# Moving SBUF tiles to 512-byte addresses, and summing the squares of a retention head on the vector engine

## The chip, the core and the metric

The kernel runs on one core of a Trainium2 chip. Its engines are TensorE (PE in the rows below; PEld is its loading of stationary operands), VectorE (DVE), ScalarE (ACT), GpSimd (POOL) and SyncE (SP), which issues most transfers. Each has its own queue of instructions, worked off in order, and they meet only at semaphores. The metric is the device time of one execution in microseconds; the median of three runs of the kernel before is 2727.9 us.

## What is computed

The reference is a trunk of four layers over 256 latent and 256 context tokens of width 1024. Layers 0 and 3 mix tokens with differential attention, layer 1 with a two-way retention of four heads, layer 2 with neighbourhood attention. Behind each mixer stands a SwiGLU network of hidden width 2816. What the change touches most is the end of a retention head:

```python
def _rms(x):
    return x32 * lax.rsqrt(jnp.mean(x32 * x32, axis=-1, keepdims=True) + EPS)
...
    def finish(o, g):
        T = o.shape[1]
        o = _rms(o).reshape(B, T, H * dv).astype(g.dtype)
        return (jax.nn.silu(g) * o) @ w_o
```

So the output `o` of a head (512 channels for each of 512 tokens) is divided by the root of its mean square and multiplied by the SiLU of a gate.

## The kernel before

All activations lie transposed: channels on the 128 partitions, tokens along the row. Weights come as a stream of 424 units of 128x1024 numbers through a ring of four slots (`RING`). For each unit SP loads `w_raw`, ACT rounds it to `w_hi` (`conv`, line 794), POOL forms the remainder `w_lo = w_raw - w_hi` (line 446), and PE multiplies in three steps, hi x hi, hi x lo and lo x hi (`three`). A unit is 8 k-tiles, so 24 matmuls of type fp32r, 512 columns wide (256 in most of layer 3). ACT may convert a unit only when PE has used the one four before it (`unit_used`), and PE takes a unit only when `lo_ready` says that POOL is done.

The stages of a layer follow one another: norm, mixer, `project`, norm, `ffn`. In the matmuls of q, k, v, gate and of the first half of the FFN the activations are `h_hi`, `h_lo`. In `project` they are `y_hi`, `y_lo` (layers 0, 2, 3) or `ry_hi`, `ry_lo` (layer 1), and in the second half of the FFN `u_hi`, `u_lo`.

A retention head (`retention`, once for each engine) is a loop of four trips with 12 units each. The order on PE is written by hand: units 0 to 3 give q and k, 4 to 7 give v, then come the scores, unit 8 and 9 (gate rows 0 and 1), the 16 products of scores and values `sT`, `rv` into banks 4 to 7, unit 10 (gate row 2), four products of the squares with a tile of ones that add up the mean square in bank 1, and unit 11 (gate row 3) into bank 3. ACT squares each of the four output tiles into one of two halves of `tmp` (line 973), converts a weight unit, takes the root as `Ln` and `Exp` (`rsqrt`, lines 813 and 814), and then loads the table of SiLU and evaluates the gates (`gate`, line 984). `gate(0)` reads bank 3, which unit 8 has filled, so unit 11 cannot write there before it. DVE forms the product in `gated` (lines 1376 and 1378).

A matmul of plain fp32 (scores, values, ones) is two records in the trace, one of fp32r is one.

SBUF tiles are laid out in the order in which they are declared. The compiled program puts `w_raw`, `w_hi`, `w_lo`, `xT`, `h_hi` and `h_lo` at addresses that leave 128 when divided by 512. Behind them stand small tiles, and so `lnm`, `ssum_rstd` and `tmp` leave 288, and `u_hi`, `u_lo`, `y_hi`, `y_lo`, `ry_hi`, `ry_lo`, `rv`, `sT`, `ada_raw` and all that share their place leave 96 (`bias`, `n_x` and `nT` leave 352). `w_*` and `h_*` thus start at a multiple of 64 bytes, the tiles behind them 32 bytes off one.

Of the kernel before, what the change touches and what calls it, by code (L numbers as in the profile page):

```python
# [127 lines left out]
class Layer:  # L128


    def __init__(self, sem, li, first_unit):
        self.li, self.kind, self.par = li, KINDS[li], li % 2
        self.n, self.nf = first_unit, first_unit + MIXER_UNITS[self.kind]

        self.zq = li < DEPTH - 1
        self.W = TOK if self.zq else SEQ
        self.na = self.kind == 2
        self.da = sum(k == 0 for k in KINDS[:li])
        self.banks = 6 if self.zq else 4
        self.groups = (3 if self.zq else 2) * (2 if self.na else 1)  # L140

        self.v_done = sem(f"v_done_{li}")
        self.v_act = sem(f"v_act_{li}")
        self.v_dve = sem(f"v_dve_{li}")
        self.s_done = sem(f"s_done_{li}")
        self.osq_ready = sem(f"osq_ready_{li}")
        self.oms_done = sem(f"oms_done_{li}")
        self.ors_ready = sem(f"ors_ready_{li}")
        self.y_ready = sem(f"y_ready_{li}")
        self.y_hi_ready = sem(f"y_hi_ready_{li}")  # L150
        self.y_lo_ready = sem(f"y_lo_ready_{li}")
        if self.kind == 1:

            self.darg_ready = sem(f"darg_ready_{li}")
            self.dexp_ready = sem(f"dexp_ready_{li}")
            self.rot_ready = sem(f"rot_ready_{li}")
            self.zcopy_ready = sem(f"zcopy_ready_{li}")
            self.sT_ready = sem(f"sT_ready_{li}")
            self.o_done = sem(f"o_done_{li}")
            self.silu_g = sem(f"silu_g_{li}")  # L160
        else:

            self.qk_dve = sem(f"qk_dve_{li}")
            self.qk_act = sem(f"qk_act_{li}")
            self.negmax = sem(f"negmax_{li}")
            self.e_ready = sem(f"e_ready_{li}")
            self.a_ready = sem(f"a_ready_{li}")
            self.t_done = sem(f"t_done_{li}")
            self.aT_ready = sem(f"aT_ready_{li}")
            self.vst_ready = sem(f"vst_ready_{li}")  # L170
            self.pv_done = sem(f"pv_done_{li}")

        self.silu_ready = sem(f"silu_ready_{li}")
        self.u_free = sem(f"u_free_{li}")
        self.u_hi_ready = sem(f"u_hi_ready_{li}")
        self.u_lo_ready = sem(f"u_lo_ready_{li}")
        self.out_done = sem(f"out_done_{li}")


def trunk(nc, xT_in, cond_in, weights, ada_w, ada_b, gains, final_g, lam_in, subln_in, decay_in,  # L180
          rpb_in, da_rope_in, ret_rope_in, ret_exp_in, na_mask_in, ident_in, out, layers=DEPTH):
    with ExitStack() as ctx:  # L182
# [4 lines left out]
            return ctx.enter_context(nc.semaphore(name))  # L187


        w_raw = sb("w_raw", [P, RING, D])  # L190
        w_hi = sb("w_hi", [P, RING, D], F32R)
        w_lo = sb("w_lo", [P, RING, D], F32R)

        xT = sb("xT", [P, KT, TOK])
        h_hi = sb("h_hi", [P, KT, TOK], F32R)
        h_lo = sb("h_lo", [P, KT, TOK], F32R)

        mod = sb("mod", [P, 2, MOD, 2])
        amp = sb("amp", [P, 2, 2, KT, 2])
        ada_sum = sb("ada_sum", [P, LOOPED, 2])  # L200
# [2 lines left out]
        gain_f = sb("gain_f", [P, KT])  # L203
        eps_c = sb("eps_c", [P, 1])
        one_c = sb("one_c", [P, 1])

        ones = sb("ones", [P, P])
        ident = sb("ident", [P, P])
        lnm = sb("lnm", [P, TOK])
        ssum_rstd = sb("ssum_rstd", [P, 2, TOK])  # L210
        ssum, rstd = ssum_rstd[:, 0, :], ssum_rstd[:, 1, :]
# [1 line left out]

        lam_sb = rstd[:, :].rearrange("p (l a d) -> p l a d", l=2, a=4)
        lam_pr = lnm[:, 0:4 * DA_DIM].rearrange("p (l a d) -> p l a d", l=2, a=2)
        lam_sum = sb("lam_sum", [P, 2, 2])
        neg_lam = sb("neg_lam", [P, 2])
        subln = sb("subln", [P, 2])
        logit = sb("logit", [P, 2 * RET_HEADS])
        lg_t = sb("lg_t", [P, 4, 2 * RET_HEADS])  # L220
        log_g = sb("log_g", [P, 2, RET_HEADS])
        lg_cur = sb("lg_cur", [P, 2])

        with ExitStack() as s:
            u_hi = sb("u_hi", [P, JT, TOK], F32R, s)
# [225 lines left out]
        def _(pe):  # L451
# [214 lines left out]
            def retention(L, q):  # L666
                with pe.Fori(0, RET_HEADS) as h:
# [36 lines left out]
                    for e in range(ET):  # L704
# [1 line left out]
                            mov, w = (sT[:, 0, kb * SEQ:kb * SEQ + SEQ], SEQ) if kb < 2 else (sT[:, kb - 1, :], TOK)  # L706
                            last = mm(bank[4 + e][:, 0:w], rv[:, kb, e * P:e * P + P], mov, j == 0, j == 3)
                        last.then_inc(L.o_done, 1)
                    head_unit(10, 2)
                    for e in range(ET):  # L710

                        pe.wait_ge(L.osq_ready, h * ET + (e + 1))
                        mm(bank[1][:, :], ones[:, :], tmp[:, e % 2, :], e == 0, e == ET - 1).then_inc(L.oms_done, 1)

                    pe.wait_ge(L.y_ready, h * ET + (ET + 1))
                    head_unit(11, 3)

            def ffn(L, q):
# [58 lines left out]
        def _(act):  # L777
# [167 lines left out]
            def retention(L):  # L945
                with own.loop(RET_HEADS, 1) as h:
# [21 lines left out]
                    for e in range(ET):  # L968
                        act.wait_ge(L.o_done, h * ET + (e + 1))
                        if e >= 2:  # L970

                            act.wait_ge(L.oms_done, h * ET + (e - 1))
                        nc.scalar.activation(tmp[:, e % 2, :], bank[4 + e][:, :], ACT.Square).then_inc(L.osq_ready, 1)
                    hconv(10)
                    act.wait_ge(L.oms_done, h * ET + ET)
                    rsqrt(TOK, bank[1][:, :], RET_V, L.ors_ready)

                    def gate(e):
# [11 lines left out]
                                             tmp[:, e % 2, :], ACT.Copy).then_inc(L.y_hi_ready, 1)  # L990

                    gate(0)
                    gate(1)
                    high(0)
                    gate(2)
# [86 lines left out]
        def _(dve):  # L1082
# [248 lines left out]
            def retention(L):  # L1331
                with own.loop(RET_HEADS, 5 + ET) as h:
# [28 lines left out]
                    for g in range(3):  # L1361
# [5 lines left out]
                                               scalar=RET_QK ** -0.5, in1=dec, op0=ALU.mult, op1=ALU.mult)\  # L1367
                            .then_inc(L.sT_ready, 1)

                    def gated(e):  # L1370

                        dve.wait_ge(L.ors_ready, h + 2)
# [8 lines left out]
                    def low(e):  # L1381
                        dve.wait_ge(L.y_hi_ready, h * ET + (e + 1))
                        V.tensor_tensor(out=row(ry_lo, h * ET + e, TOK), in0=tmp[:, e % 2, :],
                                        in1=row(ry_hi, h * ET + e, TOK), op=ALU.subtract).then_inc(L.y_lo_ready, 1)

                    gated(0)
                    for e in range(1, ET):
                        gated(e)
# [196 lines left out]
```

## Time and profile before

| | us |
|---|---|
| median of 3 runs | 2727.9 |
| lowest, highest | 2727.09, 2731.14 |
| profiled execution | 2732.85 |
| its span, first to last instruction | 2730.4 |
| PE busy in it | 2451.4 (90%) |
| DVE, POOL, ACT busy | 1344.7, 1023.0, 924.2 |

The rows come from the profiled execution. It is 4.95 us (0.18%) above the median, of which 2.45 us lie outside the span. A busy PE says that a matmul was in flight, not that it ran at its best: how many matmuls start in a stretch tells more. The granted clock is 1.00 at 2.4 GHz and 0.50 at 1.2 GHz.

### The profile page before, as it was taken

To read this page: it belongs to the slowest core of one execution; us is meant where nothing else is said; L and a number is where in the kernel's file an instruction comes from. 1 tells how busy PE (TensorE), PEld (TensorE's weight loads), DVE (VectorE), ACT (ScalarE), POOL (GpSimd) and SP (SyncE) were. 2 spreads that over 40 slices of the span, in tenths; PEclk is the share of its full clock that TensorE was granted. 3 is DMA by queue.
4 is the path that set the end of the run, shared out by engine and by line. 5 is a ranking of instruction groups with operands and counts; after the bars stand their busy time and mean duration, and the time that the engine had idled before them with its cause. 6 is when DMAs were issued, how large, how long until landed. Compare 5 with 4: busy or idle time off the path is not lost.

```text
span 2730.4 us, 34462 instructions
## 1 busy us (share of the span) xinstructions
PE 2451.4 (90%) x11378; PEld 1958.4 (72%) x11378; DVE 1344.7 (49%) x2238; ACT 924.2 (34%) x1485; POOL 1023.0 (37%) x431
## 2 busy tenths in 40 slices
PE   0639989999989999998999989999999998887998
PEld 0526668887866777686887867776788786666998
DVE  7996657664141232115766113554766513466441
ACT  2215543222232233223222223553322222354553
POOL 1212223444432332243444433223344443333786
PEclk9869999999989999999999999999999998998999
DMA  7331125554221221123655327221555422222454
GB/s 284 146 139 47 50 78 209 207 186 146 93 84 58 84 74 58 60 92 135 227 194 190 100 85 131 71 84 47 208 204 197 164 96 77 77 69 86 161 169 131
DMA packets 116393, 341.27 MB, mean 125 GB/s; under 512 B 34928, under 2 KB 36208, under 8 KB 115696
## 3 DMA queue, kind: packets, MB, share of 16 engines
q1 hardware_dynamic: 108304, 335.01, 35.9%
q10 hardware_dynamic: 8032, 5.52, 1.4%
q8 instruction: 34, 0.56, 0.1%
q14 instruction: 23, 0.19, 0.0%
HBM read 335.80 MB, written 4.69 MB: 125 GB/s over the span
## 4 chain that ended last, share of the span: by engine, by line
issue 70%; POOL 26%; PE 3%; POOLq 1%; DVE 0%; ACT 0%; DVEq 0%
POOL w_lo L446 26%; PE low_banks L453 2%; PE high_banks L453 1%; POOLq L442 0%; POOLq L445 0%; DVE xT L1507 0%; POOLq L446 0%; DVE ssum_rstd L1163 0%; DVE xT L1149 0%; ACT tmp L810 0%; ACT lnm L813 0%; ACT ssum_rstd L814 0%; DVEq L182 0%; POOL ones L439 0%; POOL eps_c L440 0%
## 5 line engine op out<-in xcount | busy, mean ns | idle before, releaser
L446 POOL TENSOR_TENSOR w_lo<-w_raw,w_hi 128x1024 fp32r<-128x1024 f32 x424 | 1022.6, 2422 | 1685.9 <-ACT w_hi L794 1685.6
L453 PE MATMUL low_banks<-h_hi,w_hi 128*128 128x512 f32 (+1 forms) x1664 | 624.5, 375 | 47.6 <-DVE h_lo L1187 23.2
L794 ACT ACTIVATE w_hi<-w_raw 128x1024 fp32r<-128x1024 f32 x424 | 444.5, 1055 | 551.2 <-PE low_banks L453 261.8
L453 PE MATMUL low_banks<-h_lo,w_hi 128*128 128x512 f32 (+1 forms) x1664 | 618.6, 372 | 0.0
L453 PE MATMUL low_banks<-h_hi,w_lo 128*128 128x512 f32 (+1 forms) x1664 | 617.6, 371 | 0.0
L453 PEld LDWEIGHTS low_banks<-h_hi,w_hi 128*128 128x128 f32 x1664 | 319.5, 192 | 115.8 <-issue 53.3
L1099 DVE SCALAR_TENSOR_TENSOR ssum_rstd<-ada_raw,high_banks 128x1024 f32<-128x1024 f32 x288 | 351.2, 1220 | 29.4 <-DMA ada_raw<-in_ada_w 20.6
L453 PEld LDWEIGHTS low_banks<-h_lo,w_hi 128*128 128x128 f32 x1664 | 319.7, 192 | 52.8 <-issue 1.0
L453 PEld LDWEIGHTS low_banks<-h_hi,w_lo 128*128 128x128 f32 x1664 | 319.2, 192 | 52.7
L1014 ACT ACTIVATE lnm<-low_banks 128x512 f32<-128x512 f32 (+1 forms) x88 | 47.8, 543 | 419.6 <-PE low_banks L453 419.6
L453 PE MATMUL high_banks<-h_hi,w_hi 128*128 128x512 f32 (+1 forms) x384 | 146.1, 381 | 14.6 <-DVE v_all L1208 9.5
L1149 DVE SCALAR_TENSOR_TENSOR xT<-low_banks,mod,xT 128x256 f32<-128x256 f32 (+1 forms) x64 | 27.8, 476 | 248.4 <-PE low_banks L453 248.4
L1416 DVE TENSOR_TENSOR tmp<-low_banks,lnm 128x512 f32<-128x512 f32 (+1 forms) x88 | 55.0, 625 | 192.5 <-ACT lnm L1014 188.5
L453 PE MATMUL high_banks<-h_lo,w_hi 128*128 128x512 f32 (+1 forms) x384 | 143.6, 374 | 0.0
L453 PE MATMUL high_banks<-h_hi,w_lo 128*128 128x512 f32 (+1 forms) x384 | 143.4, 374 | 0.0
L453 PE MATMUL low_banks<-w_hi,h_hi 128*128 128x512 f32 x192 | 79.1, 412 | 70.9 <-DVE h_lo L1187 50.7
L453 PE MATMUL high_banks<-u_hi,w_hi 128*128 (+2 forms) x352 | 130.7, 371 | 7.1 <-DVE ssum_rstd L1099 7.1
L453 PE MATMUL high_banks<-u_hi,w_lo 128*128 (+2 forms) x352 | 130.6, 371 | 0.0
L453 PE MATMUL high_banks<-u_lo,w_hi 128*128 (+2 forms) x352 | 130.4, 370 | 0.0
L453 PE MATMUL low_banks<-u_hi,w_hi 128*128 (+2 forms) x352 | 129.2, 367 | 0.0
L453 PE MATMUL low_banks<-u_hi,w_lo 128*128 (+2 forms) x352 | 129.2, 367 | 0.0
L453 PE MATMUL low_banks<-u_lo,w_hi 128*128 (+2 forms) x352 | 129.2, 367 | 0.0
(177 smaller groups left out, 3596.5 us busy)
## 6 DMA issues: line engine op xcount, KB each, us to landing
w_raw<-in_weights SPq DMA_DIRECT2D x424, 512.0 KB, 3.4
ada_raw<-in_ada_w SPq DMA_DIRECT2D x144, 512.0 KB, 3.9
ada_rest<-in_ada_w SPq DMA_DIRECT2D x8, 2048.0 KB, 7.9
ada_first<-in_ada_w SPq DMA_DIRECT2D x4, 2048.0 KB, 14.5
bias<-rpb_skew SPq DMA_DIRECT2D x64, 64.0 KB, 2.4
rpb_skew<-rpb_rows ACTq DMA_DIRECT2D x1, 3556.0 KB, 38.4
cond_l<-in_cond SPq DMA_DIRECT2D x3, 1024.0 KB, 4.6
xT<-in_xT SPq DMA_DIRECT2D x1, 2048.0 KB, 14.4
```

What stands on the lines that cost most here:

```text
L446: nc.gpsimd.tensor_tensor(out=w_lo[:, r, :], in0=w_raw[:, r, :], in1=w_hi[:, r, :], op=ALU.subtract).then_inc(lo_ready, 1)
L453: return nc.tensor.matmul(dst, lhsT, rhs, start=start, stop=stop, **kw)
L794: nc.scalar.activation(w_hi[:, r, :], w_raw[:, r, :], ACT.Copy).then_inc(hi_ready, 1)
L1014: nc.scalar.activation(lnm[:, 0:L.W], bank[2 * s][:, 0:L.W], ACT.Silu)\
L1099: last = V.scalar_tensor_tensor(out=dump, in0=w, scalar=1.0, in1=cond[:, c, :], op0=ALU.mult, op1=ALU.mult, accum_out=ada_sum[:, r, c:c + 1])
L1149: last = V.scalar_tensor_tensor(out=x, in0=src[:, c * SEQ:c * SEQ + SEQ], scalar=gate_of(L, which, m, c), in1=x, op0=ALU.mult, op1=ALU.add)
L1416: V.tensor_tensor(out=tmp[:, s, 0:L.W], in0=bank[2 * s + 1][:, 0:L.W], in1=lnm[:, 0:L.W], op=ALU.mult).then_inc(L.u_free, 1)
```

## The change

There are three edits.

1. The order of declaration: the small tiles come first, then 32 bytes of padding (`before_weights`), then the large ones. `lg_t` moves into an idle part of `lnm`. In the compiled program every large tile now starts at a multiple of 512 bytes (`bias`, `n_x`, `n_z` and `nT` at 256 beyond one).
2. In a retention head DVE adds up the four squares in `ssum` (`add_output_square`, three additions), and PE multiplies once by ones, in the middle of unit 10. ACT waits for the addition and no longer for a product before it reuses half of `tmp`.
3. ACT converts the weight unit `hconv(10)` behind the root and behind `gate(0)`, and PE's unit 11 waits for `gate(0)` itself (`silu_g`) and no longer for `gated(0)` on DVE (`y_ready`).

```diff
+        sb("before_weights", [P, 8])
+        w_raw = sb("w_raw", [P, RING, D])
...
+        lg_t = lnm[:, 4 * DA_DIM:4 * DA_DIM + 8 * RET_HEADS].rearrange("p (k a) -> p k a", k=4)
...
-                    head_unit(10, 2)
-                    for e in range(ET):
-
-                        pe.wait_ge(L.osq_ready, h * ET + (e + 1))
-                        mm(bank[1][:, :], ones[:, :], tmp[:, e % 2, :], e == 0, e == ET - 1).then_inc(L.oms_done, 1)
-
-                    pe.wait_ge(L.y_ready, h * ET + (ET + 1))
+                    unit(h * 12 + (L.n + 10), L.n + 10, bank[2], H, TOK, tiles=range(3), stop=False)
+
+                    pe.wait_ge(L.osum_step, h * (ET - 1) + (ET - 1))
+                    mm(bank[1][:, :], ones[:, :], ssum[:, :], True, True).then_inc(L.oms_done, 1)
+                    unit(h * 12 + (L.n + 10), L.n + 10, bank[2], H, TOK, tiles=range(3, KT)).then_inc(unit_used, 1)
+
+                    pe.wait_ge(L.silu_g, h * ET + 1)
                     head_unit(11, 3)
...
                         if e >= 2:

-                            act.wait_ge(L.oms_done, h * ET + (e - 1))
+                            act.wait_ge(L.osum_step, h * (ET - 1) + 1)
                         nc.scalar.activation(tmp[:, e % 2, :], bank[4 + e][:, :], ACT.Square).then_inc(L.osq_ready, 1)
-                    hconv(10)
-                    act.wait_ge(L.oms_done, h * ET + ET)
+                    act.wait_ge(L.oms_done, h + 1)
                     rsqrt(TOK, bank[1][:, :], RET_V, L.ors_ready)
...
                     gate(0)
+                    hconv(10)
                     gate(1)
...
+                    def add_output_square(e):
+
+                        dve.wait_ge(L.osq_ready, h * ET + (e + 1))
+                        if e == 1:
+                            ins = V.tensor_tensor(out=ssum[:, :], in0=tmp[:, 0, :], in1=tmp[:, 1, :], op=ALU.add)
+                        else:
+
+                            dve.wait_ge(L.osum_step, h * (ET - 1) + (e - 1))
+                            ins = V.tensor_tensor(out=ssum[:, :], in0=ssum[:, :], in1=tmp[:, e % 2, :], op=ALU.add)
+                        ins.then_inc(L.osum_step, 1)
...
+                    for e in range(1, ET):
+                        add_output_square(e)
                     gated(0)
```

On PE, at the end of a retention head in the kernel before, from the last products of `sT` and `rv` to unit 11 (the names in brackets are semaphores of layer 1):

```order
L453 MATMUL high_banks<-sT,rv 128x256 x2
L467 REGISTER_ALU
L453 MATMUL low_banks<-h_hi,w_hi 128x512 [waits lo_ready]
...
L453 MATMUL low_banks<-h_hi,w_lo 128x512
L712 REGISTER_ALU
L453 MATMUL low_banks<-tmp,ones 128x512 [waits osq_ready_1] x4
L715 REGISTER_ALU
L467 REGISTER_ALU [waits y_ready_1]
L453 MATMUL low_banks<-h_hi,w_hi 128x512 [waits lo_ready]
```

The same place on PE in the changed kernel:

```order
L456 MATMUL high_banks<-sT,rv 128x256 x2
L470 REGISTER_ALU
L456 MATMUL low_banks<-h_hi,w_hi 128x512 [waits lo_ready]
...
L456 MATMUL low_banks<-h_hi,w_lo 128x512
L456 MATMUL low_banks<-ssum_rstd,ones 128x512 [waits osum_step_1]
L456 MATMUL low_banks<-h_hi,w_hi 128x512 [waits lo_ready]
...
L718 REGISTER_ALU
L470 REGISTER_ALU [waits silu_g_1]
L456 MATMUL low_banks<-h_hi,w_hi 128x512 [waits lo_ready]
```

The product with ones has moved from behind unit 10 to behind its ninth matmul, there is one of it and no longer four, and unit 11 waits for ACT's SiLU.

On ACT, at the same place in the kernel before, from the last square to the second gate:

```order
L973 ACTIVATE tmp<-high_banks 128x512 [waits oms_done_1,o_done_1]
...
L794 ACTIVATE w_hi<-w_raw 128x1024 [waits unit_used]
L813 ACTIVATE lnm<-low_banks,eps_c 128x512 [waits oms_done_1]
...
L814 ACTIVATE ssum_rstd<-lnm 128x512 [waits act_own]
...
L984 ACT_TABLE_LOAD [waits unit_used]
L984 ACTIVATE lnm<-low_banks 128x512 [waits ors_ready_1]
L984 ACTIVATE darg<-low_banks 128x512 [waits unit_used]
```

And in the changed kernel:

```order
L976 ACTIVATE tmp<-high_banks 128x512 [waits osum_step_1,o_done_1]
L816 ACTIVATE lnm<-low_banks,eps_c 128x512 [waits oms_done_1]
...
L817 ACTIVATE ssum_rstd<-lnm 128x512 [waits act_own]
...
L986 ACT_TABLE_LOAD [waits unit_used]
L986 ACTIVATE lnm<-low_banks 128x512 [waits ors_ready_1]
...
L797 ACTIVATE w_hi<-w_raw 128x1024 [waits unit_used]
L986 ACTIVATE darg<-low_banks 128x512 [waits unit_used]
```

The conversion of a weight unit has moved from ahead of the root to between the first and the second gate.

## Rows read from the trace of the kernel before

**Rows 1.** The profile's page: span, busy time of each engine, granted clock in 40 slices.

```profile
span 2730.4 us, 34462 instructions
PE 2451.4 (90%) x11378; PEld 1958.4 (72%) x11378; DVE 1344.7 (49%) x2238; ACT 924.2 (34%) x1485; POOL 1023.0 (37%) x431
PEclk9869999999989999999999999999999998998999
```

**Rows 2.** Waits of PE during the four heads (788 to 1156 us): total, times, longest.

```profile
PE low_banks L453 <- DVE tmp L1378: 16.6, 4, 4.2
```

**Rows 3.** Timeline of PE, head 0: start us, length, instruction, idle before it.

```profile
851.00 10.48 PE L453 MATMUL high_banks<-sT,rv 128*128 128x512 f32 x32
861.13 0.58 PE L453 MATMUL low_banks<-h_hi,w_hi 128*128 128x512 f32 x1
...
866.78 3.75 PE L453 MATMUL low_banks<-tmp,ones 128*128 128x512 f32 x8
...
869.40 0.30 PEld L453 LDWEIGHTS low_banks<-tmp,ones 128*128 128x128 f32 x2 [0.56 <-ACT tmp L973]
...
874.68 0.79 PE L453 MATMUL low_banks<-h_hi,w_hi 128*128 128x512 f32 x1 [4.15 <-DVE tmp L1378]
```

**Rows 4.** Timeline of ACT, head 0.

```profile
853.78 0.60 ACT L973 ACTIVATE tmp<-high_banks 128x512 f32<-128x512 f32 x1 [1.52 <-PE high_banks L453]
856.36 0.60 ACT L973 ACTIVATE tmp<-high_banks 128x512 f32<-128x512 f32 x1 [1.98 <-PE high_banks L453]
...
867.90 0.60 ACT L973 ACTIVATE tmp<-high_banks 128x512 f32<-128x512 f32 x1 [10.94 <-PE low_banks L453]
868.76 0.60 ACT L973 ACTIVATE tmp<-high_banks 128x512 f32<-128x512 f32 x1 [0.26 <-PE low_banks L453]
869.25 1.05 ACT L794 ACTIVATE w_hi<-w_raw 128x1024 fp32r<-128x1024 f32 x1
870.57 0.69 ACT L813 ACTIVATE lnm<-low_banks,eps_c 128x512 f32<-128x512 f32 x1 [0.27 <-PE low_banks L453]
871.29 0.63 ACT L814 ACTIVATE ssum_rstd<-lnm 128x512 f32<-128x512 f32 x1
871.93 1.28 ACT L984 ACT_TABLE_LOAD   x1
873.23 0.60 ACT L984 ACTIVATE lnm<-low_banks 128x512 f32<-128x512 f32 x1
```

**Rows 5.** Timelines of DVE and POOL, head 0.

```profile
871.95 0.69 DVE L1376 TENSOR_TENSOR ssum_rstd<-high_banks,ssum_rstd 128x512 f32<-128x512 f32 x1 [30.96 <-ACT ssum_rstd L814]
873.86 0.69 DVE L1378 TENSOR_TENSOR tmp<-ssum_rstd,lnm 128x512 f32<-128x512 f32 x1 [1.22 <-ACT lnm L984]
...
852.33 2.35 POOL L446 TENSOR_TENSOR w_lo<-w_raw,w_hi 128x1024 fp32r<-128x1024 f32 x1 [3.05 <-ACT w_hi L794]
870.38 2.35 POOL L446 TENSOR_TENSOR w_lo<-w_raw,w_hi 128x1024 fp32r<-128x1024 f32 x1 [15.70 <-ACT w_hi L794]
```

**Rows 6.** Windows at the slow clock: length, PE busy (count), granted clock, DMA share, GB/s.

```profile
874.68:879.85 5.17, 5.17 (x12) 0.50 0.18 72
965.95:972.01 6.06, 6.06 (x14) 0.50 0.14 56
1057.62:1060.75 3.13, 3.13 (x7) 0.50 0.26 105
1147.92:1152.92 5.00, 5.00 (x12) 0.50 0.17 67
```

**Rows 7.** Windows in stages without a wait, same columns.

```profile
660.00:760.00 100.00, 100.00 (x431) 1.00 0.29 95
1160.00:1240.00 80.00, 80.00 (x344) 1.00 0.25 85
420.00:640.00 220.00, 219.68 (x969) 1.00 0.57 203
815.00:830.00 15.00, 15.00 (x68) 1.00 0.38 125
2656.00:2716.00 60.00, 60.00 (x509) 1.00 0.46 149
2611.00:2616.00 5.00, 5.00 (x44) 1.00 0.44 154
```

**Rows 8.** One addition of squares beside POOL, behind the FFN of layer 0 (timeline).

```profile
776.76 2.42 DVE L1163 TENSOR_TENSOR ssum_rstd<-ssum_rstd,tmp 128x512 f32<-128x512 f32 x1 [0.71 <-ACT tmp L810]
776.28 2.34 POOL L446 TENSOR_TENSOR w_lo<-w_raw,w_hi 128x1024 fp32r<-128x1024 f32 x1 [3.27 <-ACT w_hi L794]
```

More of the change, by code:

```diff
@@ L160, in __init__ @@
             self.silu_g = sem(f"silu_g_{li}")
+            self.osum_step = sem(f"osum_step_{li}")
         else:
@@ L187, in sem @@
             return ctx.enter_context(nc.semaphore(name))
[L190 to L196, printed above, removed]
         mod = sb("mod", [P, 2, MOD, 2])
@@ L208, in trunk @@
         ident = sb("ident", [P, P])
+        lam_sum = sb("lam_sum", [P, 2, 2])
+        neg_lam = sb("neg_lam", [P, 2])
+        subln = sb("subln", [P, 2])
+        logit = sb("logit", [P, 2 * RET_HEADS])
+        log_g = sb("log_g", [P, 2, RET_HEADS])
+        lg_cur = sb("lg_cur", [P, 2])
+        sb("before_weights", [P, 8])
+        w_raw = sb("w_raw", [P, RING, D])
+        w_hi = sb("w_hi", [P, RING, D], F32R)
+        w_lo = sb("w_lo", [P, RING, D], F32R)
+        xT = sb("xT", [P, KT, TOK])
+        h_hi = sb("h_hi", [P, KT, TOK], F32R)
+        h_lo = sb("h_lo", [P, KT, TOK], F32R)
         lnm = sb("lnm", [P, TOK])
@@ L215, in trunk @@
         lam_pr = lnm[:, 0:4 * DA_DIM].rearrange("p (l a d) -> p l a d", l=2, a=2)
[L216 to L222, printed above, removed]
+        lg_t = lnm[:, 4 * DA_DIM:4 * DA_DIM + 8 * RET_HEADS].rearrange("p (k a) -> p k a", k=4)
         with ExitStack() as s:
```

## The prediction, made before the changed kernel ran

> **What bounds the kernel now.** I read the page first: PE has a matmul in flight for 2451.4 of 2730.4 us, and no other engine is busy for half of the span [rows 1]. So a change helps if it shortens PE's own stream, fills one of its gaps, or keeps its clock up. I then asked for PE's waits within the retention heads. There is one kind: unit 11 waits four times for `gated(0)`, 4.15 us each [rows 2, 3]. The timeline of a head shows what lies in front of that wait. Third, I laid windows over stretches in which PE never stops, and counted matmuls: that gives the pitch from one start to the next, which a busy share of 100% hides [rows 7].
>
> **The end of a head, before.** From the first matmul of unit 10 (861.13) to the first of unit 11 (874.68) are 13.55 us [rows 3]. Unit 10 is 24 matmuls at 0.2268 us, 5.44 us. The other 8.1 us are four products with ones, which ACT's third and fourth square must come between (`tmp` has two halves, and PE comes to the first product only behind unit 10, so the third square starts at 867.90 after 10.94 us of idling), and then the chain weight conversion, `Ln`, `Exp`, table, SiLU, `gated(0)` [rows 3 to 5].
>
> **The same place, after.** The products of `sT` and `rv` still end at 861.13. The squares no longer wait for PE: they follow the four outputs, 2.58 us apart [rows 4], so at about 853.8, 856.4, 858.9 and 861.5. DVE, idle for 30.96 us here [rows 5], adds at about 857.0, 859.6 and 862.1, 0.69 us each (the length of row 871.95), done at 862.8. PE starts unit 10 at 861.13 and has nine matmuls to do before the product: 863.17. The sum is there 0.4 us earlier, so no stall. The product is 2 records of 0.43 us, 0.86 us; from its first start to `Ln` take 1.06 us, as for the last product before (its tile of ones is loaded from 869.40, the product follows 0.1 us later, and `Ln` comes at 870.57 [rows 3, 4]). `Ln` then starts at 864.23. From the start of `Ln` to the end of the first SiLU are 873.83 - 870.57 = 3.26 us [rows 4], and the conversion is out of that chain: SiLU ends at 867.49. PE's other 15 matmuls of unit 10 end at 863.17 + 0.86 + 3.40 = 867.43. Unit 11 needs the usual 0.13 us from release to start (873.86 + 0.69 = 874.55 to 874.68 [rows 3, 5]): 867.65. Gain: 7.03 us a head, **28.1 us** for four.
>
> What is late next? `hconv(10)` starts at about 867.5 (its wait is for unit 10) and not at 869.25, so no weight is later. `hconv(10)` stands ahead of `gate(1)`, whose product must be in before the next head writes banks 0 and 1. `gate(1)` ends at about 869.2, and POOL's subtraction (868.6 to 871.0) may hold DVE's second factor until 871.7. Unit 11 lasts until 873.1, so 1.4 us are left. Units 2 and 3 of the next head come 11 us later still. The three additions cost DVE 8.3 us in all, in its idle stretch. Without that cover each would put up to 0.69 us into the chain.
>
> **The clock.** Behind each of the four waits PE runs at a granted clock of 0.50, which is 1.2 GHz, for 5.17, 6.06, 3.13 and 5.00 us [rows 6]. The matmuls there start 0.427 us apart and not 0.227. So of these 19.36 us a share of 1 - 0.2268/0.427 = 0.47 is lost, **9.1 us**. In the 13.55 us before, PE had been idle for 4.15 us in one piece and for shorter ones between the products. After the change the longest gap that I work out is 0.2 us. I take all 9.1; the other end is 0, if the clock falls all the same.
>
> **The addresses.** In windows without a stall, (length + 0.4)/count is the pitch (0.4 us is one matmul, since one in flight at the edge is counted). With `u_*` and `ry_*` as moving operand: 100.4/431 and 80.4/344, together 233.3 ns. With `h_*`: 15.4/68 = 226.5 and 220.1/969 = 227.1 ns, so 226.8 [rows 7]. Clock, width and weight tiles are alike. What differs is that `u_*` and `ry_*` start 32 bytes off a multiple of 64, and `h_*` on one. At 256 columns the sign turns: `u_*` 60.3/509 = 118.5 ns, `h_*` 5.3/44 = 120.5 ns. After the change all lie on a multiple of 64, like `h_*` now, so I take the price of `h_*`. The count: `u_*` 22 units of 24 in each of four layers, `y_*` 8 units in layers 0, 2 and 3, `ry_*` 16 units. 512 wide are 3x528 + 2x192 + 384 = 2352 matmuls, gain 2352 x 6.5 ns = 15.3 us. 256 wide are 528 + 192 = 720, loss 720 x 2.0 = 1.4 us. Net **13.9 us**, all on PE's path, since these stages have no other bound (a unit is 5.4 us on PE at 512 columns, POOL's part 2.35 [rows 5]). The bounds: 0, if the difference comes from the stage and not from the address, and 41 us, if aligned tiles go down to what plain fp32 rows show. There, 16 pairs of a 512- and a 256-wide product at two passes, 24,576 columns, take from 10.13 to 10.48 us [rows 3], so 512 columns take 211 to 218 ns, and 2352 x (233.3 - 215.8) = 41. I stay with 226.8, the nearest row. For DVE, ACT, POOL and the transfers no row shows a cost that goes with the address: DVE takes 0.69 us for 512 fp32 on tiles that leave 288 and on banks alike [rows 5]. I cost them at nothing, and leave 3 us either way for the start of the program, where PE waits for DVE.
>
> **Sum.** 28.1 + 9.1 + 13.9 = 51.1 us. The profiled execution of 2732.85 us would become 2681.7, and the median of 2727.9 us, 0.18% lower, **2676.8 us**.
>
> **The rivals.** A: the layout is worth nothing, because the two pitches belong to the stages. For it: `u_*` and `h_*` never stand in the same stage. Against it: the second half of the FFN in layer 0 and `project` of layer 1 agree on 233 [rows 7], though other work stands beside them. Only the heads count, 37.2 us: 2690.7. Chance 0.13. The Trainium skill (SBUF — State Buffer, in the part on Door 1) says that SBUF has 16-byte cachelines and that a stretch of consecutive elements runs at full bandwidth. Both old and new addresses are multiples of 16, so by this rule the address would cost nothing and A would hold; 233.3 beside 226.8 ns speaks against it.
>
> B: offset 128 costs too. The 226.8 ns of `h_*` are 13.5 ns above 512 columns at 2.4 GHz, at 256 columns 13.8, the same constant, and fp32 rows do not show it. If it goes away at a multiple of 512, the `h_*` matmuls gain as well. Of 10,176 fp32r matmuls (424 x 24), 3072 are counted above; of the 7104 left 1248 are 256 wide. Gain on top of my forecast: 226.8 - 215.8 = 11 ns for all 10,176, 112 us, less some 7% at the slow clock or behind other bounds, 104 us. Time: 2573. Against it: the constant may as well belong to the change of stationary operand in this type, and then no address helps. Chance 0.17. By the Trainium skill (TensorE: Matmul & The Clock Gate, on the back-to-back gap) a warm matmul of N columns starts N/2.4 + 2.5 ns after the one before, 215.7 ns at 512; by it B's gain would be estimated at the same size, and no fp32r row here reaches it.
>
> C: an addition meets POOL. Row 776.76 shows one of 0.69 us stretched to 2.42, until POOL's subtraction of 776.28 ends [rows 8]. In the heads POOL's last one ends at 854.7 and the first addition comes at 857.0 [rows 5], so it should not. If it does in each head, PE stalls up to 1.7 us: 7 us, perhaps with the clock lost, 2684 to 2693. Chance 0.05. The Trainium skill (SBUF — State Buffer, on who interferes with whom) says that a DVE instruction with two SBUF inputs contends with a POOL instruction that reads SBUF; rows 8 agree.
>
> D, on the other side: the common phase of stationary and moving tile is what costs, and at a multiple of 512 it is one step dearer than today's best. The step seen is 6.5 ns. One step on the 5856 `h_*` matmuls costs 38 us and eats the heads' gain: 2729 with `u_*` unchanged, which is no change. Two steps on them and one on the rest, 76 + 15, give 2782. It decides from 6.4 ns on `h_*`. No row shows such a step at an address that both tiles share. Chance 0.03, and 0.02 for the one step.
>
> **How the numbers follow.** My forecast has 0.60, with 2665 to 2688 of its own. A and C lie above it, and the head's chain may be half a microsecond longer, or the clock kept only in part: up to 2696. Below it, 2647 is the heads with 41 us for the layout and the 3 us of the start; I go to 2645. 2645 to 2696 leaves out B and D, about 0.2. A difference of 0.2% (5.5 us) is about what can be told from no change here. Faster by more than that: 0.60 + 0.13 + 0.17 + 0.05 = 0.95. Within it 0.02, slower 0.03.
>
> **What would show it.** In the trace after: PE's wait for `gated(0)` gone, and at most 0.3 us ahead of unit 11. Four products with ones in layer 1 (8 records) and not 16. The granted clock at 1.00 throughout the four heads, behind the first 10 us of layer 1. DVE's additions at 0.69 us each. A window of the second half of the FFN, 100 us long, with 442 or 443 matmuls (431 before): 431 is rival A, 465 is B. The stretch of `h_*` with 969 matmuls in 220 us should stay at 969; more is B, fewer is D. I am wrong about the heads if unit 11 starts more than 7 us behind the start of unit 10.

## The result and the profile after

The changed kernel takes 2677.4 us (median of 4 runs, 2675.9 to 2680.6) against 2727.9 us (2727.1 to 2731.1) for the kernel before: a ratio of 0.981, 95% interval 0.980 to 0.9825. The forecast was 2676.8 us. Its profiled execution took 2677.65 us; the span fell from 2730.4 to 2675.4 us.

The page of the kernel after, against [rows 1] (busy us, share, instructions; then the granted clock in 40 slices):

```profile
span 2675.4 us, 34434 instructions
PE 2417.5 (90%) x11354; PEld 1949.2 (73%) x11354; DVE 1362.0 (51%) x2250; ACT 924.5 (35%) x1485; POOL 1026.4 (38%) x431
PEclk9869999999989999999999989999999998998999
```

PE's busy time fell by 34 us, with 24 records fewer. DVE got 12 instructions and 17 us more: 8.3 us are the three additions in each of four heads, 7.0 us are four products that last longer beside POOL (below), and the other 2 I didn't follow. By stage, layer 1's mixer went from 466.8 to 426.5 us, 40.3 us less. The rest is 14.7 us shorter in sum, not evenly: layer 0's FFN 376.8 us for 382.6, layer 2's FFN 377.9 for 382.3, but layer 3's mixer 221.6 for 217.9. Around its beginning (2225 to 2312 us) the clock was at 0.50 for 23.9 us in this execution, and for 13.7 in that of before; such stretches come and go from kernel to kernel.

Now a head. Start us, length, instruction, idle before it, on PE, in head 0; in [rows 3] the unit behind the products with ones waited 4.15 us:

```profile
852.94 0.58 PE L456 MATMUL low_banks<-h_hi,w_hi 128*128 128x512 f32 x1
853.36 0.40 PE L456 MATMUL low_banks<-h_lo,w_hi 128*128 128x512 f32 x1
...
855.19 1.02 PE L456 MATMUL low_banks<-ssum_rstd,ones 128*128 128x512 f32 x2
855.65 0.80 PE L456 MATMUL low_banks<-h_hi,w_hi 128*128 128x512 f32 x1
...
859.24 0.39 PE L456 MATMUL low_banks<-h_hi,w_lo 128*128 128x512 f32 x1
859.64 0.49 PE L456 MATMUL low_banks<-h_hi,w_hi 128*128 128x512 f32 x1
```

Unit 10 starts at 852.94, unit 11 at 859.64: 6.70 us where it was 13.55, and the same in the other three heads. Unit 10's last matmul starts at 859.24 and would let the next one start at 859.47; the gap is 0.17 us. On ACT, in place of [rows 4]:

```profile
853.33 0.60 ACT L976 ACTIVATE tmp<-high_banks 128x512 f32<-128x512 f32 x1 [1.98 <-PE high_banks L456]
856.25 0.69 ACT L816 ACTIVATE lnm<-low_banks,eps_c 128x512 f32<-128x512 f32 x1 [2.32 <-PE low_banks L456]
856.97 0.63 ACT L817 ACTIVATE ssum_rstd<-lnm 128x512 f32<-128x512 f32 x1
857.62 1.28 ACT L986 ACT_TABLE_LOAD   x1
858.92 0.60 ACT L986 ACTIVATE lnm<-low_banks 128x512 f32<-128x512 f32 x1
859.67 1.06 ACT L797 ACTIVATE w_hi<-w_raw 128x1024 fp32r<-128x1024 f32 x1 [0.15 <-PE low_banks L456]
```

From the start of `Ln` (856.25) to the end of SiLU (859.52) are 3.27 us, with no conversion among them. On DVE and POOL, in place of [rows 5]:

```profile
861.32 2.44 DVE L1392 TENSOR_TENSOR tmp<-ssum_rstd,darg 128x512 f32<-128x512 f32 x1 [0.35 <-ACT darg L986]
...
860.81 2.40 POOL L449 TENSOR_TENSOR w_lo<-w_raw,w_hi 128x1024 fp32r<-128x1024 f32 x1 [14.32 <-ACT w_hi L797]
```

And the second and third addition of all four heads, on line 1381 (duration in ns, lowest, median, highest; first and last start); the first, on line 1377, takes as long:

```profile
L1381 DVE TENSOR_TENSOR ssum_rstd<-ssum_rstd,tmp x8: 691/692/693, 851.4 to 1099.9; 128x512 f32<-128x512 f32 x8
```

The additions take 0.69 us. The conversion that moved brings POOL's subtraction with it, and that meets DVE's second factor: 2.44 us and not 0.69. Nothing of it reaches PE. Between 780 and 1150 us PE has one wait left (total, times, longest), in place of [rows 2]. It is the one for the norm with which layer 1 begins, 5.0 us in the kernel before too; from 782 to 1200 us there is none:

```profile
PE low_banks L456 <- DVE h_lo L1190: 5.0, 1, 5.0
```

Windows of the kernel after (length, busy (count) of PE, PEld, DVE, ACT, POOL, granted clock, DMA share, GB/s): the four heads from the first end of a head on, then the stages of [rows 7], shifted by what had been gained by then. The moving operand is `u_*`, `ry_*`, `h_*`, and `u_*` at 256 columns:

```profile
850.00:1150.00 300.00, 299.95 (x1248) 233.93 (x1247) 101.30 (x132) 102.25 (x137) 107.64 (x44) 1.00 0.22 75
655.00:755.00 100.00, 100.00 (x443) 82.83 (x442) 7.59 (x12) 21.29 (x22) 45.13 (x19) 1.00 0.29 100
1115.00:1195.00 80.00, 80.00 (x355) 66.24 (x353) 13.40 (x23) 20.16 (x23) 35.81 (x16) 1.00 0.25 85
418.00:638.00 220.00, 220.00 (x972) 182.14 (x971) 153.83 (x240) 63.66 (x83) 97.38 (x41) 1.00 0.58 203
2602.00:2662.00 60.00, 60.00 (x503) 60.00 (x502) 7.07 (x9) 21.97 (x24) 47.07 (x20) 1.00 0.45 148
```

The clock stays at 1.00 through the heads, where [rows 6] has four stretches at 0.50. `u_*` has 443 matmuls in 100 us (431 before), `ry_*` 355 in 80 us (344), `h_*` 972 in 220 us (969, where PE had 0.3 us of waits), and 256 wide `u_*` is slower, 503 in 60 us (509).

### The profile page after: what moved, and what is told of

It reads as the page before. It is cut to its first block, busy times and chain, and to the rows that moved or that the text cites. A ratio compares the mean times of both kernels' runs of the same rounds, so it can differ in the third digit from the quotient of the medians.

```text
span 2675.4 us, 34434 instructions
## 1 busy us (share of the span) xinstructions
PE 2417.5 (90%) x11354; PEld 1949.2 (73%) x11354; DVE 1362.0 (51%) x2250; ACT 924.5 (35%) x1485; POOL 1026.4 (38%) x431
## 4 chain that ended last, share of the span: by engine, by line
issue 49%; POOL 20%; PE 19%; DVE 8%; ACT 2%; DMA 1%; POOLq 0%; DVEq 0%; SPq 0%; ACTq 0%
POOL w_lo L449 20%; PE low_banks L456 13%; PE high_banks L456 6%; DVE dump L1102 3%; DVE tmp L1179 1%; DVE h_lo L1190 1%; ACT e_x L856 1%; DVE rot L1221 1%; DVE ssum_rstd L1166 0%; ACT e_z L862 0%; DMA ada_first<-in_ada_w 0%; DVE mod L1110 0%; ACT lnm L816 0%; DVE a_x L1276 0%; ACT ssum_rstd L817 0%
## 5 line engine op out<-in xcount | busy, mean ns | idle before, releaser
L797 ACT ACTIVATE w_hi<-w_raw 128x1024 fp32r<-128x1024 f32 x424 | 444.4, 1056 | 533.4 <-PE low_banks L456 260.1
L456 PEld LDWEIGHTS low_banks<-h_lo,w_hi 128*128 128x128 f32 x1664 | 316.8, 190 | 53.1 <-issue 1.9
## 6 DMA issues: line engine op xcount, KB each, us to landing
rpb_skew<-rpb_rows ACTq DMA_DIRECT2D x1, 3556.0 KB, 36.5
```

The source lines that it names most:

```text
L456: return nc.tensor.matmul(dst, lhsT, rhs, start=start, stop=stop, **kw)
L797: nc.scalar.activation(w_hi[:, r, :], w_raw[:, r, :], ACT.Copy).then_inc(hi_ready, 1)
```

## The experiments

Where nothing else is said a kernel is the changed one with one edit. For a second kind of evidence beside windows, I took from each trace the mean distance between the starts of neighbouring matmuls of one kind at a granted clock of 1.00; a "pitch" below is that.

### Each half alone

`layout_only` is the kernel before with the new order of declaration. `heads_only` is the changed kernel with the old one.

> The kernel before with the new order of SBUF tiles alone, every large tile at a multiple of 512 bytes. My theory: a matmul with u, y or ry as moving operand starts 226.8 ns after the one before and not 233.3, at 256 columns 120 and not 118.5, so 13.9 us less: about 2714 us, and the four waits of unit 11 stay at 4.15 us. Rival A (the pitch belongs to the stage): 2728 us. A third reading, that the whole gain of 50.5 us is not the sum of two independent parts: less than 2710 or more than 2720 here while the heads alone give 2691.

> The changed kernel with the old order of SBUF tiles: only the sum on DVE, the single product with ones and the later weight conversion. My theory: 28 us from the 13.55 us at the end of each head and 9 us from the clock, 2691 us; no window at 1.2 GHz in the heads. Rival (the slow clock comes anyway, at some point of a head): 2700 us. The pitch with u, y and ry stays at 233.

Measured beside the same runs of the kernel before (2730.1 us): 2713.8 us for the layout (ratio 0.995, 0.9936 to 0.9963) and 2693.2 us for the heads (0.9868, 0.9853 to 0.9883). By the medians the halves are worth 16.2 and 36.9 us, 53.1 in all. The change gained 50.5 beside its own runs of the kernel before (2727.9), and would have gained 52.7 beside 2730.1. By the ratios they are worth 0.50% and 1.32%, together 1.82%, against 1.88% for the change. So they add up within what the runs can tell, and neither needs the other. The 16.2 us are the looser number: of the five runs with the new layout three took 2712.9 to 2713.8 us, at a mean granted clock of 0.965 to 0.966, and two took 2718.3 and 2719.0, at 0.963. The ratio makes it 13.6 us. In `heads_only` the window of `u_*` still has the old count, so the pitch goes with the layout alone:

```profile
660.00:760.00 100.00, 100.00 (x430) 80.50 (x430) 7.60 (x12) 21.27 (x22) 43.25 (x18) 1.00 0.29 95
```

### The conversion ahead of the root again

```diff
+                    hconv(10)
                     act.wait_ge(L.oms_done, h + 1)
                     rsqrt(TOK, bank[1][:, :], RET_V, L.ors_ready)
...
                     gate(0)
-                    hconv(10)
```

> The changed kernel with one edit undone: ACT converts the weight unit again ahead of the root. The conversion waits for the end of unit 10, so Ln starts at about 868.5 in the times of the forecast and not at 864.2; unit 11 comes 4.3 us later in each head, 17 us in all. My theory of the clock (it falls behind a stall of this size) adds about 9 us: 2704 us. Rival (the slow clock of the kernel before came from the broken stretch of products and squares, not from the stall): 2694 us.

2703.8 us (2702.7 to 2705.8): 26.4 us of the gain are gone. ACT in head 0, then the unit behind it on PE, then all of PE's waits in the heads, then a window behind one of them:

```profile
860.93 1.06 ACT L797 ACTIVATE w_hi<-w_raw 128x1024 fp32r<-128x1024 f32 x1 [5.74 <-PE low_banks L456]
861.90 0.67 ACT L816 ACTIVATE lnm<-low_banks,eps_c 128x512 f32<-128x512 f32 x1
...
865.26 0.49 PE L456 MATMUL low_banks<-h_hi,w_hi 128*128 128x512 f32 x1 [4.37 <-ACT lnm L987]
PE low_banks L456 <- ACT lnm L987: 17.5, 4, 4.4
951.00:958.00 7.00, 4.82 (x11) 3.81 (x12) 5.50 (x9) 4.26 (x7) 1.33 (x1) 0.52 0.23 75
```

ACT takes its work in order. It stands idle for 5.74 us until PE has freed the weight slot, at the end of unit 10, and `Ln`, whose input came in the middle of unit 10, stands behind the conversion. So three things in the edit to the heads (one product with ones, its early place, the wait for `silu_g`) give 10.0 us without the fourth, the place of the conversion (2713.8 in `layout_only` less 2703.8). The clock fell here with one product with ones in place of four, so it was not the broken stretch of products and squares that brought it down, as the rival in the expectation had it.

### Unit 11 waits for DVE's factor

```diff
-                    pe.wait_ge(L.silu_g, h * ET + 1)
+                    pe.wait_ge(L.y_ready, h * ET + (ET + 1))
```

> The changed kernel with unit 11 waiting for gated(0) on DVE as before, instead of for the SiLU. The product of DVE ends 0.75 us behind the SiLU, so PE waits 0.8 us a head, 3 us in all, if so short a gap leaves the clock at 2.4 GHz: 2680 us. Rival (any wait in this place costs the clock too): 2689 us.

2681.4 us (2679.7 to 2683.3), 4.0 us over the changed kernel:

```profile
PE low_banks L456 <- DVE tmp L1392: 3.0, 4, 0.7
```

Four waits of 0.7 us, and the clock stays at 1.00 behind them. The difference from `conv_ahead` is 22.4 us. 14.5 of them are idle time (17.5 - 3.0); the other 7.9 us are left for the clock, which falls to 0.50 behind each of the four waits of 4.4 us and behind none of the four of 0.7. A count gives about the same: in the heads of `conv_ahead` 44 matmuls start in stretches at 0.50, 0.427 us apart and not 0.227, which is 8.8 us.

### Which address counts

Four kernels move tiles by padding. `at_480` and `at_64` move all large tiles together, to 480 and to 64 bytes beyond a multiple of 512; `w_off` moves the weight tiles alone, to 480; `h_off` moves `h_*` to 32 and what is declared behind them (`u_*`, `y_*`, `ry_*`) to 64.

```diff
         sb("before_weights", [P, 8])
+        sb("before_h", [P, 8])
         h_hi = sb("h_hi", [P, KT, TOK], F32R)
         h_lo = sb("h_lo", [P, KT, TOK], F32R)
+        sb("behind_h", [P, 8])
```

> The changed kernel with all large tiles moved 32 bytes down: every one of them leaves 480 when divided by 512, so none is at a multiple of 64, and stationary and moving tiles lie alike. If the place of the moving tile itself counts, the pitch is 233 ns for h as well as for u, y and ry, and the time 2677 + 8208 x 6.5 ns = 2730 us (less what 256 columns give back, 2 us). If only the distance between stationary and moving tile counts, the pitch stays at 227 and the time at 2677.

> The changed kernel with all large tiles 64 bytes up, at multiples of 64 but not of 128. If 64 bytes are what counts, pitch 227 ns and 2677 us. If multiples of 128 are wanted, a pitch of more than 227 and over 2690 us.

> The changed kernel with the three weight rings alone moved 32 bytes down (480), all activations at multiples of 512. Weights are the stationary operand nearly everywhere, and the moving one only where v is formed (960 matmuls). If the moving tile's place counts: 227 ns, but 233 where v is formed, 6 us: 2683. If the distance or the stationary tile's place counts: 233 everywhere, 2728 us.

> The changed kernel with h_hi and h_lo alone 32 bytes off (they leave 32), weights at 0, all tiles behind them at 64. If the moving tile's place counts, 233 ns in the units of q, k, gates and the first half of the FFN (about 4900 matmuls of 512 columns), 227 elsewhere: 2677 + 32 - 2 = 2707 us, and 227 where v is formed, since there h is the stationary operand. If the stationary tile's place counts: 233 only where v is formed, 2683.

One run each: 2678.9, 2681.0, 2718.8 and 2708.4 us. With 480 for all, nothing is lost; with 480 for the weights alone, 41.5 us are. `at_64` has the pitches of the changed kernel too (226.7 ns with `u_*`, 226.9 with `h_*`). Windows of `at_480` (`u_*`, `h_*`), `w_off` (the same) and `h_off` (`u_*`, `ry_*`, `h_*`), in this order:

```profile
660.00:760.00 100.00, 100.00 (x443) 82.84 (x442) 7.60 (x12) 21.87 (x23) 44.59 (x19) 1.00 0.29 97
420.00:640.00 220.00, 220.00 (x971) 181.99 (x970) 152.84 (x241) 62.19 (x81) 97.87 (x42) 1.00 0.57 203
```

```profile
660.00:760.00 100.00, 100.00 (x430) 80.31 (x430) 8.95 (x14) 21.27 (x22) 44.15 (x19) 1.00 0.29 100
420.00:640.00 220.00, 220.00 (x945) 176.72 (x944) 150.84 (x236) 60.61 (x79) 95.08 (x40) 1.00 0.57 203
```

```profile
660.00:760.00 100.00, 100.00 (x438) 82.05 (x438) 8.59 (x14) 21.29 (x22) 44.16 (x19) 1.00 0.30 100
1125.00:1205.00 80.00, 80.00 (x351) 65.62 (x350) 17.95 (x29) 21.53 (x25) 34.40 (x15) 1.00 0.28 92
420.00:640.00 220.00, 220.00 (x944) 176.73 (x943) 147.00 (x236) 60.28 (x79) 95.66 (x40) 1.00 0.57 203
```

In `w_off` `h_*` lies where it lay, at a multiple of 512, and its count falls from 972 to 945. In `h_off` `u_*` lies at a multiple of 64 and still loses 5 matmuls in 100 us. So neither the moving tile's address nor its remainder by 64 decides, and `at_480` excludes the stationary tile's address. The distance between the moving and the stationary tile does. `w_off` came 9 us under the 2728 expected for that case: the pitch went to 233.3 ns everywhere at 512 columns, but down to 117 at 256.

### Eight distances

`phases_a` leaves the weights at 0 and puts `h_*` at 128, `u_*` at 256, `y_*` at 192 and `ry_*` at 384; `phases_b` has `h_*` at 64, `u_*` at 160, `y_*` at 96, `ry_*` at 448.

```diff
+        sb("before_h", [P, 32])
...
+            sb("before_u", [P, 32], F32, s)
             u_hi = sb("u_hi", [P, JT, TOK], F32R, s)
```

> The runs so far say that the distance between the moving and the stationary tile counts: 0 gives 226.7 ns at 512 columns and 120.0 at 256, 32 bytes either way gives 233.3, and 64 (u, y and ry in h_off) gives 228.9. Here four distances at once in the changed kernel, weights at 0: h at 128, u at 256, y at 192, ry at 384. If only the place within a 64-byte line counted, all would be 226.7, but h_off already speaks against that. If the distance counts modulo 128: 226.7 for h, u and ry and 228.9 for y. Modulo 256: 226.7 for u alone. If distance 0 is the best place there is, no pitch is under 226.7 and the time is 2677 or more. If 0 is the worst of the even places, some pitch goes towards 216 and the time falls to 2600 or less.

> As the run before, with the distances h 64, u 160, y 96, ry 448, weights at 0. If the distance counts modulo 128: 228.9 ns for h and ry, 233.3 for u and y, time 2677 + 4900 x 2.2 ns + 1584 x 6.6 ns + others, about 2705. If every odd multiple of 32 gives 233.3, u and y show it in either case.

2706.8 and 2706.5 us, one run each. Windows of `phases_a`, then of `phases_b` (`u_*`, `ry_*`, `h_*`):

```profile
660.00:760.00 100.00, 100.00 (x442) 82.79 (x442) 10.58 (x16) 23.98 (x25) 45.52 (x19) 1.00 0.31 103
1125.00:1205.00 80.00, 80.00 (x344) 64.36 (x344) 15.99 (x27) 21.26 (x25) 34.06 (x14) 1.00 0.26 88
420.00:640.00 220.00, 220.00 (x948) 178.38 (x947) 150.72 (x236) 61.14 (x80) 96.06 (x40) 1.00 0.58 203
```

```profile
660.00:760.00 100.00, 100.00 (x428) 80.41 (x427) 7.61 (x12) 21.10 (x22) 43.15 (x18) 1.00 0.29 95
1125.00:1205.00 80.00, 80.00 (x345) 64.49 (x344) 16.49 (x28) 21.09 (x25) 34.08 (x14) 1.00 0.28 92
420.00:640.00 220.00, 220.00 (x963) 180.54 (x962) 151.64 (x237) 61.66 (x81) 96.08 (x40) 1.00 0.57 203
```

The distance has a direction. Where v is formed the same two tiles change roles, with the weights as moving and `h_*` as stationary operand. In `phases_b` `h_*` lies 64 bytes beyond the weights: as moving operand it has 228.9 ns, but the 96 matmuls of v in head 0 start 233.3 ns apart, as at a distance of 192. In the changed kernel they start 226.7 ns apart. Windows in that unit of work, of the changed kernel and of `phases_b`:

```profile
805.50:825.50 20.00, 20.00 (x90) 16.57 (x89) 3.87 (x6) 4.79 (x6) 10.31 (x5) 1.00 0.36 124
817.00:837.00 20.00, 20.00 (x88) 16.11 (x87) 3.52 (x6) 4.22 (x5) 9.61 (x4) 1.00 0.32 106
```

All pitches together, in ns, by the distance from the stationary to the moving tile:

| bytes, modulo 256 | 512 columns | 256 columns | from |
|---|---|---|---|
| 0 | 226.7 to 227.1 | 119.7 to 120.0 | all tiles alike; `u_*` at 256 |
| 32 | 233.3 | 116.7 to 117.3 | `w_off`, `h_*` in `h_off` |
| 64 | 228.9 | 117.1 (`h_*`), 117.8 (`u_*`) | `phases_b`, `h_off` |
| 96 | 233.3 | 119.9 | `y_*` in `phases_b` |
| 128 | 232.6, 233.3 (`ry_*` at 384) | 118.8 | `phases_a` |
| 160 | 234.3 | 117.3 | `u_*` in `phases_b` |
| 192 | 233.2, 233.3 (`ry_*` at 448) | 114.5 | `y_*` in `phases_a` |
| 224 | 233.3 | 118.3 | the kernel before (`u_*` at 96, weights at 128) |

At 512 columns a distance of 0 is the best that was seen, and 256 (`u_*` in `phases_a`) is as good as 0. 128 isn't (232.6), and 192 has 233.3 ns where 64 has 228.9, so a period of 128 is excluded; that of 256 rests on three pairs (0 and 256, 128 and 384, 192 and 448), of which only the first says much, since most distances have 233. At 256 columns it is the worst, with 96. No distance came near the 215.8 ns that rival B counted on.

### Two edits beyond the change

What is left on PE's path beside its own stream? Over the whole span it sits idle for `ssum_rstd`, the sum of squares ahead of a norm, for 70.1 us, 31.3 of them in one piece at the start of the program (the first line below, of the kernel after). The end of layer 0's FFN in that kernel shows why (ACT, POOL, DVE, PE):

```profile
  DVE ssum_rstd L1166: 70.1, 9
...
767.30 1.06 ACT L797 ACTIVATE w_hi<-w_raw 128x1024 fp32r<-128x1024 f32 x1 [0.56 <-PE low_banks L456]
768.44 2.34 POOL L449 TENSOR_TENSOR w_lo<-w_raw,w_hi 128x1024 fp32r<-128x1024 f32 x1 [3.10 <-ACT w_hi L797]
768.91 2.42 DVE L1166 TENSOR_TENSOR ssum_rstd<-ssum_rstd,tmp 128x512 f32<-128x512 f32 x1 [0.65 <-ACT tmp L813]
...
773.56 2.08 PE L456 MATMUL high_banks<-ssum_rstd,ones 128*128 128x512 f32 x2 [6.36 <-DVE ssum_rstd L1166]
```

It is the pattern of [rows 8]: a conversion whose product nobody needs yet starts POOL's subtraction beside an addition in the chain that PE waits for. It also stands ahead of a square on ACT, for which DVE waits 0.65 us. `late_convs` puts the last conversion behind the last square, at the end of each FFN and of `project` in layers 0, 2 and 3:

```diff
-                conv(n + JT + AHEAD - 1)
                 for m in range(5, 8):
                     square(e0 + m + 1, m, L.W, m % 2)
+                conv(n + JT + AHEAD - 1)
```

> The changed kernel with ACT's last weight conversion behind the last square at the end of each FFN (three times) and of project in layers 0, 2 and 3. In the trace of the changed kernel that conversion takes 1.06 us ahead of the square, and it lets POOL start, whose subtraction then holds the addition of squares on DVE for 2.42 us instead of 0.69. Behind the FFN the gap on PE should go from 6.7 to about 4.0 us, behind project from 4.6 to 3.1 (as in layer 1, where the conversion already stands behind the square). 3 x 2.7 + 3 x 1.5 = 12.6 us: 2665 us. Rival (the next norm then finds ACT busy with the conversion, and the time only moves): no gain, 2677.

2662.1 us (2660.6 to 2663.4; ratio 0.9752, 0.9739 to 0.9766), 15.3 us below the changed kernel. The wait over the span, and DVE's last two additions with POOL and PE behind them:

```profile
  DVE ssum_rstd L1170: 57.6, 9
...
771.59 1.48 DVE L1170 TENSOR_TENSOR ssum_rstd<-ssum_rstd,tmp 128x512 f32<-128x512 f32 x2
773.12 2.08 PE L456 MATMUL high_banks<-ssum_rstd,ones 128*128 128x512 f32 x2 [3.89 <-DVE ssum_rstd L1170]
773.36 2.34 POOL L449 TENSOR_TENSOR w_lo<-w_raw,w_hi 128x1024 fp32r<-128x1024 f32 x1 [6.00 <-ACT w_hi L797]
```

POOL starts when the additions are over. This wait is 2.47 us shorter: 1.73 are the addition that was held (2.42 - 0.69), 0.65 the wait for the square behind the conversion. Of the 15.3 us the wait for the sum accounts for 12.5 in all. The other 3 are most likely the clock: with the same 11354 records PE is busy for 2413.6 us and not 2417.5, and the mean granted clock is 0.971 to 0.973 in all five runs, against 0.968 to 0.969 in the four of the changed kernel. No run shows this part by itself.

`narrow_192` tries the table's 114.5 ns: in layer 3, whose products are 256 wide, `y_*`, `u_*` and the FFN's `h_*` are kept 48 columns further along in their tiles, on top of `late_convs`.

```diff
+        self.S = 0 if self.zq else 48
...
-                                     (h_hi[:, k, 0:W], h_lo[:, k, 0:W]), k == 0, k == KT - 1)
+                                     (h_hi[:, k, S:S + W], h_lo[:, k, S:S + W]), k == 0, k == KT - 1)
```

> late_convs, and in layer 3, where the products are 256 columns wide, h_* in the FFN, u_* and y_* are written and read 48 columns (192 bytes) further along in their tiles, so that the moving operand starts 192 bytes beyond a multiple of 256 while the weight tiles stay at a multiple of 512. In phases_a the only 256-wide matmuls at a distance of 192 bytes, y_* in layer 3, start 114.5 ns apart, against 119.8 at a distance of 0. If the distance sets the pitch at 256 columns whatever the stage, the FFN of layer 3 gains 1056 x 5.3 (h_*) + 528 x 5.5 (u_*) and project 192 x 5.3 ns, 9.5 us in all: 2652.5 us, with a pitch of 114.5 for all three. If the 114.5 belongs to project of layer 3, only y_* moves: 2661. The widths of 512 must stay at 226.7 to 226.9 in both.

2658.7 us (2653.5 to 2663.1; ratio 0.9735, 0.9721 to 0.9749). That is 3.4 us below `late_convs`, not 9.5, and the intervals overlap. Second half of layer 3's FFN in `late_convs` and in `narrow_192`, and PE's waits for POOL in the first half, in the same order:

```profile
2588.00:2648.00 60.00, 60.00 (x502) 60.00 (x501) 7.00 (x11) 21.43 (x23) 46.51 (x20) 1.00 0.44 145
PE low_banks L456 <- POOL w_lo L449: 6.7, 10, 0.7
```

```profile
2588.00:2648.00 60.00, 60.00 (x511) 60.00 (x511) 7.96 (x11) 22.57 (x25) 47.52 (x20) 1.00 0.45 149
PE low_banks L457 <- POOL w_lo L450: 8.9, 10, 1.0
```

`u_*` has 117.8 ns now and not 114.5, `y_*` 116.9, `h_*` in the FFN 115.4. So the direction carries from stage to stage, the size doesn't: the distance isn't all that sets the pitch at this width. And in the first half a unit now ends before POOL has the next weights, so 2.2 us come back as waits. By these pitches the gain is 1056 x 4.5 + 528 x 2.2 + 192 x 2.9 ns = 6.5 us, less 2.2: an estimate of 4.3 us, beside 3.4 measured.

## Why the prediction was right

**The heads.** Forecast: 7.03 us a head, 28.1. The trace has 13.55 - 6.70 = 6.85 in each of the four heads, 27.4 us. The links of the chain held: squares 2.58 us apart, additions 0.69, the product from its first start to `Ln` 1.06, `Ln` to SiLU 3.27 (3.26), the gap ahead of unit 11 0.17 (0.2). One was sized too low: the nine matmuls ahead of the product take 2.25 us and not 2.04, since the second of them starts 0.42 us behind the first (852.94 to 853.36) and not 0.227. That accounts for the 0.18 us by which the forecast of a head was off.

**The clock.** Forecast: 9.1 us, by rows at either level. The stretches at 0.50 are gone from the heads. `conv_ahead`, in which they are back, costs 7.9 us more than its idle time explains, and 8.8 by a count of matmuls; the same count in the kernel before is 45 matmuls, 9.0 us. With 27.4 this is 35.3 to 36.5 us, against 37 measured for `heads_only` and 40.3 in the trace of layer 1's mixer, where the addresses of `ry_*` gave 2.5. From unit 10 of one head to that of the next the traces have 91.27, 91.66 and 90.31 us before and 81.98, 81.97 and 81.97 after: 9.1 us a head, where the two terms of the forecast make 9.3.

**The addresses.** Forecast: 13.9 us. Measured: 16.2 in `layout_only` by the medians and 13.6 by the ratio (10 to 17.5 by its interval), and 15.9 between `heads_only` and the changed kernel. By the pitches it is 14.1: 2352 matmuls at 226.8 and not 233.3 ns, 720 at 119.9 and not 118.3. The counts came as given: 443 (442 or 443), `h_*` at 972 with 969 expected. (Single stages differ more, as layer 3's mixer above shows; the sum is what the runs confirm.) What failed is the reason that the step gave. It said that `u_*` and `ry_*` pay for lying 32 bytes off a multiple of 64. At 480, which is 32 off, they pay nothing once the weights lie there too, and in `h_off`, on a multiple of 64, they pay 2.2 ns. The rows ahead of the prediction could not tell these apart: there `h_*` and the weights were both at 128, so "on a multiple of 64" and "at the weights' own phase" were the same tiles. The number was right since after the change both hold, and since the `h_*` rows that gave the price were rows at a distance of 0. That part of the forecast was luck: by its reason `ry_*` at 448 in `phases_b`, a multiple of 64, would have cost nothing, and it has 233.3 ns.

**The rivals.** A (the layout is worth nothing) fell with `layout_only`. The Trainium skill (SBUF — State Buffer, Door 1) says that SBUF has 16-byte cachelines and that consecutive accesses to one such line have full bandwidth. The prediction drew from it that all multiples of 16 bytes cost the same. For one tile's address the runs agree, since `at_480` loses nothing. For two tiles of one matmul the inference fails: all addresses here are multiples of 16, and there are 226.7 and 233.3 ns. B (offset 128 costs too) fell: 128, 0, 64 and 480 give the same pitch if all share them. Its 215.8 ns, which is also the upper bound's, lies within the 211 to 218 ns that the prediction read from the fp32 products, but is no row itself. C (an addition meets POOL) didn't happen in the heads. D asked whether a phase that both tiles share could cost a step. It was the right variable, with the sign the other way: a shared phase is the best one, and the kernel before had it for `h_*` already.

**What was said to come next** came: POOL's subtraction holds DVE's second factor (2.44 us) and no stall follows. The same meeting elsewhere was worth more than the prediction saw. It used [rows 8] only to price a risk of the change. The row stood on PE's path, at the end of a stage, and taking that conversion away gave 15.3 us, more than the whole layout. The Trainium skill (SBUF — State Buffer, on who interferes with whom) says that a DVE instruction with two SBUF inputs contends with one of GpSimd that reads SBUF. The rows agree: 0.69 us alone, 2.42 beside POOL.

## What to carry over

Before moving work off a chain, ask of every instruction that stands in an in-order engine's queue ahead of it what it waits for: one conversion that nobody needed yet was worth 26 us here, and others of its kind at the ends of stages, which held DVE by way of POOL and of ACT's queue, another 15. If one tile's address seems to cost something, move the two tiles of a pair together and apart before a rule is made of it. And a cheaper pitch on PE is only worth something where no other engine is the next to be late.

## What the runs showed of the hardware

- Matmuls of 512 fp32r columns start 226.7 to 227.1 ns apart if moving and stationary tile lie at the same offset modulo 256 bytes, and 228.9 to 234.3 ns at the other distances tried. Which offset they share (0, 64, 128, 480) makes no difference. The direction counts: 228.9 ns with the moving tile 64 bytes beyond the stationary one, 233.3 with it 64 bytes short of the stationary one.
- At 256 columns the order turns: 119.7 to 120.0 ns at a distance of 0, 114.5 to 119.9 elsewhere. The same distance of 192 bytes gave 114.5 in one kernel and 116.9 in another for `y_*`. Why is open, and so is what in the chip makes the distance count.
- In the retention heads a wait of 0.7 us on PE leaves the granted clock at 1.00 (4 of 4), and one of 4.4 us is followed by 3.4 to 6.8 us at 0.50 (4 of 4), as those of 4.15 us are in the kernel before (4 of 4). No run has a wait between 0.7 and 4.1 us in this place.
- A DVE product or addition with two SBUF inputs takes 0.69 us alone, and 2.42 to 2.44 beside a POOL subtraction of 2.3 to 2.4 us; it ends 0.55 us behind POOL's end.
